# Attention scores of each head in a PSUM bank of their own, and the turned probabilities in two banks

## The chip, the cores and the metric

One core of a Trainium2 chip runs the kernel. The time is the device time of one execution in microseconds (us). The kernel before has a median of 2364.11 us in three runs (2362.43 to 2365.06).

## What is computed

One hybrid encoder layer is applied with the same weights to two sequences of 256 and 1024 tokens, of width 1024. A windowed attention branch (16 query heads in 4 groups, head width 64, window 128) and a bidirectional mLSTM branch run on the same normalised input; a gated merge, a projection, and a gated feed-forward follow. The attention is all that the change touches:

```python
def block_fn(args):
    j, qj, kj, vj = args
    kpos = j * BLOCK - BLOCK + jnp.arange(3 * BLOCK)
    valid = in_window & ((kpos >= 0) & (kpos < S))[None, :]
    s = jnp.einsum('bqgrd,bkgd->bgrqk', qj.astype(F32), kj.astype(F32)) * scale + alibi
    s = jnp.where(valid, s, -jnp.inf)
    sink_col = jnp.broadcast_to(sink_g[None, :, :, None, None], s.shape[:-1] + (1,))
    p = jax.nn.softmax(jnp.concatenate([s, sink_col], axis=-1), axis=-1)[..., :-1]
    o = jnp.einsum('bgrqk,bkgd->bqgrd', p, vj.astype(F32))
    return o.astype(qj.dtype)
```

## The kernel before

Tokens stand on the free axis in most of the program; both sequences are joined into 1280 tokens, ten blocks of 128. A group of four query heads with its one key and value head, and one mLSTM head, are done together: this is "a head" below, `h` = 0 to 3. For each, `mlstm(h)` runs first and `attend(h)` after it. Beside the attention of heads 0 to 2 TensorE (PE) computes dense input products of the next mLSTM head, two groups in each block (`M_BESIDE`); beside head 3 it computes late gate products (`late_group`) in block 0 and products of the mLSTM branch (`branch_m`, table `B_BESIDE`) from block 1 on.

Numbers are carried as a high part and a low part (a "split"): the high part is a rounded copy that ScalarE (ACT) writes, the low part the difference that VectorE (DVE) subtracts.

A block `j` sees two key blocks at a sequence's edge (`j` = 0, 1, 2, 9) and three inside (`j` = 3 to 8). For a block, in the order of the data:

- PE, `a_scores(j)` (matmul at L3653): for each of the four query heads `r`, a product with the high and with the low keys. `S_AT` says at which column of three joined PSUM banks (2, 3, 4) a head's scores begin: at 0, 384, 768 and 1152. A bank holds 512 columns, so heads 1 and 2 lie across a bank's end and are written in two pieces each.
- DVE, `scores_max(j)` (L2727, L2730): adds the distance term and takes the maximum; `exp_bias(j)` (L2735 to L2740). It writes `prob`, so it waits until the probabilities of block `j - 1` have been turned (`a_t`).
- ACT, `exps(j)` (L2340), then DVE, `normalise(j)` (L2752), one count of `a_p` for each query head.
- PE, `a_turn(j)` (transposes at L3673): each key block's probabilities are turned, four transposes into one bank; banks 6, 7 and 5 for the first, second and third key block (`TURN_BANK`). The scores of the next block stand between the second and the third turn (in edge blocks after the second). Bank 5 is also where the values' product is summed, so before the third turn PE waits for `a_o`, the last read of bank 5 by block `j - 1`.
- ACT, `evac_pt(j)` (L2348) writes the high part of each turned block, and DVE, `split_probs(j)` (L2813), the low part, after `scores_max(j + 1)` and `exp_bias(j + 1)`.
- PE: the dense groups beside the block, then `a_values(j)` (L3686, L3687) into bank 5.
- ACT, `evac_o(j)` (L2375), reads one half of the sum, DVE, `add_out(j)` (L2819), adds the other half and counts `a_o`.

Each engine does its own list in the order written. On ACT `evac_pt(j)` stands behind `evac_o(j - 1)` and what follows that: in heads 0 to 2, from block 4 to 7, two tanh gates (`gate_o`, L2168); in head 3, behind `evac_o(2)`, the eight copies of `ym_hi(2)` (L2397). In block 0 of head 3 the eight copies of `ym_hi(0)` stand just ahead of `evac_pt(0)`, and `ym_hi(1)`, two `evac_late` (L2093) and `evac_o(0)` follow `exps(1)`. GpSimd (POOL) takes the low parts of `ym_hi` (L1525) before `branch_m` may use them.

Of the kernel before, what the change touches and what calls it, by code (L numbers as in the profile page):

```python
# [24 lines left out]
P = 128  # L25
# [4 lines left out]
NB = T // P  # L30
# [3 lines left out]
HD = 64  # L34
QPG = 4
# [116 lines left out]
RAW = {"B11": 9, "B21": 10, "B22": 11, "B12": 12}  # L152


S_AT = [3 * P * r for r in range(4)]


COLS_AT = 9
# [41 lines left out]

LAST_AHEAD = 3

TURN_BANK = [6, 7, 5]

CHUNKS = [(0, 256), (256, 768), (768, T)]

# [243 lines left out]
def lin(f, h):  # L450

    if isinstance(h, int):
        return f(h)
    a, b = f(0), f(1)
    assert f(2) == 2 * b - a
    return h * (b - a) + a if b != a else a


def build(nc, w, wdn, xt, cols, bvo, sink, outs):
# [36 lines left out]
    prob_h = at("prob_h", 159808, [P, 3, QPG * P], F32R)  # L496
    prob_l = at("prob_l", 199392, [P, 3, QPG * P], F32R)
    ya_st = at("ya_st", 165952, [HD, QPG, P])
# [121 lines left out]
    ps = nc.alloc_psum_tensor("ps", [P, 8, 512], F32)  # L620
# [73 lines left out]
    a_t = sem("a_probs_transposed")  # L694
# [164 lines left out]
    def kblocks(j):  # L859
        lo, hi = seq_of(j)  # L860
        return list(range(max(lo, j - 1), min(hi, j + 2)))
# [5 lines left out]
    def tiles_before(j):  # L867

        return sum(len(kblocks(n)) for n in range(j))

    def score_at(j, r):

# [67 lines left out]
    with ctx_block as block:  # L940
# [1116 lines left out]
        def _(act):  # L2057
# [285 lines left out]

            def evac_pt(j, h):

                act.wait_ge(a_t, lin(lambda k: NB * k + j + 1, h))
                for n in range(len(kblocks(j))):
                    nc.scalar.activation(prob_h[:, n], ps[:, TURN_BANK[n], :], ACT.Identity).then_inc(a_pt, 1)  # L2348

            def split_keys(h):  # L2350
# [19 lines left out]
            def evac_o(j, h):  # L2370

                act.wait_ge(a_v, lin(lambda k: NB * k + j + 1, h))
                if j > 0:
                    act.wait_ge(s_ya, lin(lambda k: 16 * (NB * k + j), h))
                nc.scalar.activation(ya_st[:], ps[HD:P, 5, :].rearrange("p (r t) -> p r t", r=QPG),  # L2375
                                     ACT.Copy).then_inc(a_oc, 1)

            def store_o(j, h):
# [99 lines left out]
        def _(dve):  # L2478
            V = nc.vector
# [238 lines left out]
            def scores_max(j, h):  # L2718

                kb = kblocks(j)  # L2720
                a, b = (kb[0] - j + 1) * P, (kb[-1] - j + 2) * P
                dve.wait_ge(a_s_done, lin(lambda k: NB * k + j + 1, h))
                flat = ps[:, 2:5, :].rearrange("p b t -> p (b t)")
                if j > 0:
                    dve.wait_ge(a_t, lin(lambda k: NB * k + j, h))
                for r in range(QPG):
                    V.scalar_tensor_tensor(prob[:, r, a:b], absrel[:, a:b], slope8[:, bass.ds(h * QPG + r, 1)],  # L2727
                                           flat[:, score_at(j, r) + a:score_at(j, r) + b], ALU.mult, ALU.add)
                dve.drain()
                V.tensor_reduce(small[:, 16:20], prob[:, :, a:b], AX.X, ALU.max)  # L2730
# [72 lines left out]
                                           q_st[j > 0][rows, odd].bitcast(F32), ALU.subtract)  # L2803
                last.then_inc(a_ql, 1)

            def split_probs(j, h):

                if j == 0:
                    for s in range(2):
                        dve.wait_ge(s_gs[s], gates_stored(h))  # L2810
                for n in range(len(kblocks(j))):
                    dve.wait_ge(a_pt, lin(lambda k: tiles_before(NB) * k + tiles_before(j) + n + 1, h))
                    last = V.tensor_tensor(prob_l[:, n], ps[:, TURN_BANK[n], :], prob_h[:, n].bitcast(F32),  # L2813
                                           ALU.subtract)
                last.then_inc(a_pl, 1)

            def add_out(j, h):
                dve.wait_ge(a_oc, lin(lambda k: NB * k + j + 1, h))
                V.tensor_tensor(ya_st[:], ya_st[:], ps[0:HD, 5, :].rearrange("p (r t) -> p r t", r=QPG),  # L2819
                                ALU.add).then_inc(a_o, 1)  # L2820

            def attend(h, dense):
                dve.drain()
                split_keys(0, h)
                split_query(0, h)
                split_values(h)
                dve.wait_ge(m_y, lin(lambda k: 5 * (k + 1), h))
                scores_max(0, h)
                exp_bias(0, h)
                split_keys(1, h)  # L2830
                split_query(1, h)
                normalise(0, h)
                for j in range(NB):

                    if j + 1 < NB:
                        scores_max(j + 1, h)
                        exp_bias(j + 1, h)
                    ahead = B_BESIDE[j][:1] if not dense and len(B_BESIDE[j]) == 3 else []
                    for n in ahead:
                        gate_product(n)  # L2840
                    split_probs(j, h)
                    if j + 2 < NB:
                        split_query(j + 2, h)
                    vo = [g - 12 for g in M_BESIDE[j] if dense and g >= 12]
                    for blk in vo[:1]:
                        evac_vo(blk, h, 1)
                    if j + 1 < NB:
                        normalise(j + 1, h)
                    for blk in vo[1:]:
                        evac_vo(blk, h, 1)  # L2850
                    if not dense and j == 0:
                        ym_lo_last()
                    if not dense:
                        for n in B_BESIDE[j][len(ahead):]:
                            gate_product(n)
                    add_out(j, h)
                if not dense:
                    ya_lo(0)
                    gate_product(NBR - 2)
                    ya_lo(1, range(3))  # L2860
                    gate_product(NBR - 1)
                    ya_lo(1, range(3, KT))
                    ya_lo(2)

                dve.wait_ge(m_ye, lin(lambda k: 5 * (k + 1), h))
# [493 lines left out]
        def _(pe):  # L3359
# [278 lines left out]
            def a_scores(j, h):  # L3638

                kb = kblocks(j)  # L3640
                a, b = (kb[0] - j + 1) * P, (kb[-1] - j + 2) * P
                if j in (0, NB_A):
                    pe.wait_ge(a_kl, 2 * h + 1 + (j > 0))
                if j:
                    pe.wait_ge(a_m, lin(lambda k: NB * k + j, h))
                pe.wait_ge(a_ql, lin(lambda k: NB * k + j + 1, h))
                for r in range(QPG):
                    lo = score_at(j, r) + a
                    while lo < score_at(j, r) + b:
                        hi = min(score_at(j, r) + b, (lo // 512 + 1) * 512)  # L3650
                        k0 = (j - 1) * P + lo - score_at(j, r)
                        for n, keys in enumerate((kk_h, kk_l)):
                            ins = mm(ps[:, 2 + lo // 512, lo % 512:lo % 512 + hi - lo], q_st[j > 0][:, r % 2, r // 2],  # L3653
                                     keys[:, k0:k0 + hi - lo], start=n == 0, stop=n == 1)
                        lo = hi
                ins.then_inc(a_s_done, 1)

            def a_turn(j, h):


                if j == 0:
                    pe.wait_ge(a_av, lin(lambda k: k + 1, h))
                kb = kblocks(j)
                for n, blk in enumerate(kb):
                    o = (blk - j + 1) * P
                    if n == 2:
                        if j + 1 < NB:
                            a_scores(j + 1, h)
                        pe.wait_ge(a_o, lin(lambda k: NB * k + j, h))
                    for r in range(QPG):  # L3670
                        if n == 0:
                            pe.wait_ge(a_p, QPG * (NB * h + j) + r + 1)
                        ins = nc.tensor.transpose(ps[:, TURN_BANK[n], r * P:(r + 1) * P], prob[:, r, o:o + P], ident[:])  # L3673
                ins.then_inc(a_t, 1)
                if len(kb) < 3 and j + 1 < NB:
                    a_scores(j + 1, h)

            def a_values(j, h):

                pe.wait_ge(a_pl, lin(lambda k: NB * k + j + 1, h))  # L3680
                kb = kblocks(j)
                if len(kb) < 3 and j > 0:
                    pe.wait_ge(a_o, lin(lambda k: NB * k + j, h))
                for n, blk in enumerate(kb):
                    vals = v_block(blk).rearrange("p s e -> p (s e)")
                    mm(ps[:, 5, :], vals, prob_h[:, n], start=n == 0, stop=False)  # L3686
                    ins = mm(ps[:, 5, :], vals, prob_l[:, n], start=False, stop=n == len(kb) - 1)  # L3687
                ins.then_inc(a_v, 1)

            def branch_m(n):  # L3690
# [526 lines left out]
```

## Time and profile before

| | before |
|---|---|
| median of the runs | 2364.11 us (2362.43 to 2365.06) |
| the profiled execution's own time | 2362.85 us |
| its span, first to last instruction | 2361.0 us |
| PE busy | 2328.4 us, 99% of the span |
| DVE, ACT, POOL busy | 65%, 39%, 54% |
| share of PE in the chain that ended last | 81% |
| scores, L3653, in 28 to 53% of the span | 416 matmuls |
| granted TensorE clock, mean | 0.999 |

A matmul's row shows a start and a modelled end; the next one starts before that end, so the pace of PE is read from start to start, and a busy share of 99% does not say that it ran at its peak. In a timeline, rows of one kind that follow each other are merged into one (x8), with the time from the first start to the last end.

### The profile page before, as it was taken

Reading aid. Unit: us, or ns where it says so; the run is one execution under the profiler, and the core shown is the slowest. Engines: PE = TensorE matmul, PEld = TensorE weight load, DVE = VectorE, ACT = ScalarE, POOL = GpSimd, SP = SyncE. Lnnn points to the kernel's source line nnn. Section 1 sums busy time; section 2 is a strip of 40 time slices with the busy share of each in tenths; the row PEclk is TensorE's granted clock in tenths of the full one; section 3 lists DMA queues with packets and bytes.
Section 4 is the critical chain, followed back from the end, with each engine's and each line's share of the span. In section 5 each row is a group of like instructions: output and inputs, shape, how many; then the busy total and the mean of one; then the engine's idle time right before and its main releaser. Section 6 shows DMA issues by size and latency. Waiting matters only on the chain.

```text
span 2361.0 us, 37054 instructions
## 1 busy us (share of the span) xinstructions
PE 2328.4 (99%) x13662; PEld 2104.9 (89%) x13662; DVE 1544.0 (65%) x2731; ACT 909.3 (39%) x1886; POOL 1276.2 (54%) x1548
## 2 busy tenths in 40 slices
PE   7999999999999999999999999999999999999998
PEld 6888888888888888888888899999999999989887
DVE  6734467555674547755786633999878788866447
ACT  5212444224442244324644112554433334542433
POOL 3365522555225651345443548797555555976677
PEclk9999999999999999999999999999999999999999
DMA  3132211321113211223454443332444434488873
GB/s 140 52 110 90 71 37 28 113 92 51 37 41 110 92 52 32 73 82 125 130 165 163 140 152 124 125 111 90 156 146 141 157 130 151 136 287 272 283 232 121
DMA packets 186956, 285.64 MB, mean 121 GB/s; under 512 B 14344, under 2 KB 126824, under 8 KB 186776
## 3 DMA queue, kind: packets, MB, share of 16 engines
q1 hardware_dynamic: 139320, 241.97, 31.1%
q10 hardware_dynamic: 47456, 41.31, 5.8%
q8 instruction: 109, 1.79, 0.3%
q14 instruction: 71, 0.58, 0.1%
HBM read 203.46 MB, written 79.68 MB: 120 GB/s over the span
## 4 chain that ended last, share of the span: by engine, by line
PE 81%; DVE 8%; DMA 4%; DVEq 2%; POOL 2%; ACT 1%; issue 1%; SPq 1%; ACTq 0%; POOLq 0%
PE ps L3373 15%; PE ps L3374 15%; PE ps L3375 15%; PE ps L3388 3%; PE ps L3384 3%; PE ps L3385 3%; PE ps L3438 3%; PE ps L3439 3%; PE ps L3440 3%; PE ps L3653 2%; PE ps L3673 2%; PE ps L3555 2%; PE ps L3944 2%; PE ps L3946 2%; PE ps L3945 2%; DMA weight_sum_scratch<-s_stage 1%
## 5 line engine op out<-in xcount | busy, mean ns | idle before, releaser
L3373 PE MATMUL ps<-ht_h,unit_h 128*128 128x512 f32 (+1 forms) x1408 | 502.5, 357 | 1.5 <-POOL unit_l L1434 0.8
L3375 PE MATMUL ps<-ht_h,unit_l 128*128 128x512 f32 (+1 forms) x1408 | 498.4, 354 | 0.0
L3374 PE MATMUL ps<-ht_l,unit_h 128*128 128x512 f32 (+1 forms) x1408 | 498.3, 354 | 0.0
L1412 POOL TENSOR_TENSOR unit_h<-unit_raw,colt 128x256 fp32r<-128x256 f32 x320 | 209.4, 684 | 275.5 <-DMA unit_raw<-w 275.1
L3373 PEld LDWEIGHTS ps<-ht_h,unit_h 128*128 128x128 f32 x1408 | 266.1, 189 | 37.9 <-POOL unit_l L1434 1.8
L3375 PEld LDWEIGHTS ps<-ht_h,unit_l 128*128 128x128 f32 x1408 | 265.9, 189 | 37.5
L3374 PEld LDWEIGHTS ps<-ht_l,unit_h 128*128 128x128 f32 x1408 | 266.2, 189 | 35.0 <-issue 0.2
L1416 POOL TENSOR_TENSOR unit_l<-unit_raw,unit_h 128x256 fp32r<-128x256 f32 x320 | 246.7, 802 | 11.7 <-issue 0.4
L1584 POOL TENSOR_TENSOR unit_l<-unit_raw,unit_h 128x256 fp32r<-128x256 f32 x164 | 158.5, 991 | 92.5 <-DVE unit_raw L3023 92.5
L1584 POOL TENSOR_TENSOR sum_l<-sum_raw,sum_h 128x256 fp32r<-128x256 f32 x132 | 139.5, 1076 | 86.8 <-DVE sum_raw L3030 74.7
L1505 POOL TENSOR_TENSOR v_high<-v_raw,colt 128x256 fp32r<-128x256 f32 x40 | 27.0, 675 | 231.5 <-DVE o_st L2526 231.5
L2340 ACT ACTIVATE prob<-prob,small 128x384 f32<-128x384 f32 (+1 forms) x160 | 89.8, 563 | 112.4 <-DVE small L2740 112.3
L1624 POOL TENSOR_TENSOR block_l<-block_raw,block_h 128x256 fp32r<-128x256 f32 x120 | 106.7, 925 | 47.9 <-ACT block_h L1955 47.8
L3384 PE MATMUL ps<-operands,unit_h 128*128 128x320 f32 x420 | 125.3, 310 | 0.2 <-DVE kept_products L3179 0.2
L3385 PE MATMUL ps<-operands,unit_h 128*128 128x320 f32 x420 | 124.7, 309 | 0.0
L3438 PE MATMUL ps<-unit_h,ht_h 128*128 128x512 f32 x312 | 123.2, 395 | 0.0
L2727 DVE SCALAR_TENSOR_TENSOR prob<-absrel,slope,ps 128x384 f32<-128x384 f32 (+1 forms) x160 | 79.0, 556 | 65.8 <-PE ps L3673 38.2
L3440 PE MATMUL ps<-unit_h,ht_l 128*128 128x512 f32 x312 | 121.6, 390 | 0.0
L3439 PE MATMUL ps<-unit_l,ht_h 128*128 128x512 f32 x312 | 121.5, 389 | 0.0
L3122 DVE TENSOR_TENSOR side<-side_raw,side 128x1536 fp32r<-128x1536 f32 (+2 forms) x40 | 65.7, 1676 | 53.2 <-ACT side L1860 53.2
L3373 PE MATMUL ps<-operands,unit_h 128*128 128x320 f32 x320 | 99.1, 310 | 0.2
L3374 PE MATMUL ps<-operands,unit_h 128*128 128x320 f32 x320 | 98.9, 309 | 0.0
(441 smaller groups left out, 6414.0 us busy)
## 6 DMA issues: line engine op xcount, KB each, us to landing
unit_raw<-w SPq DMA_DIRECT2D x149, 512.0 KB, 3.7
bw<-exponent_rows_scratch ACTq DMA_DIRECT2D x40, 256.0 KB, 3.6
down_raw<-wdn SPq DMA_DIRECT2D x24, 384.0 KB, 4.5
side_raw<-side_sum_scratch SPq DMA_DIRECT2D x24, 384.0 KB, 6.4
block_raw<-weight_sum_scratch SPq DMA_DIRECT2D x16, 576.0 KB, 4.3
gate_scratch<-g_st SPq DMA_DIRECT2D x28, 256.0 KB, 2.2
stage<-f_scratch SPq DMA_DIRECT2D x28, 256.0 KB, 3.0
side_sum_scratch<-stage SPq DMA_DIRECT2D x14, 512.0 KB, 2.9
```

The source lines that it names most:

```text
L1412: nc.gpsimd.tensor_tensor(unit_h[:, slot, k:k + 2], unit_raw[:, slot, k:k + 2], one_col.unsqueeze(2).to_broadcast([P, 2, P]), ALU.mult)
L1416: last = nc.gpsimd.tensor_tensor(unit_l[:, slot, k:k + 2], unit_raw[:, slot, k:k + 2], unit_h[:, slot, k:k + 2].bitcast(F32), ALU.subtract)
L1584: last = nc.gpsimd.tensor_tensor(lo[:, k:k + 2], raw[:, k:k + 2], hi[:, k:k + 2].bitcast(F32), ALU.subtract)
L1624: last = nc.gpsimd.tensor_tensor(blk_l[n][:, a:b], blk_raw[n][:, a:b], blk_h[n][:, a:b].bitcast(F32), ALU.subtract)
L3373: mm(out_ap, wh, hi(k + k_first), start=first and k == 0, stop=False, skip_group_check=skip)
L3374: mm(out_ap, wh, lo(k + k_first), start=False, stop=False, skip_group_check=skip)
L3375: ins = mm(out_ap, wl, hi(k + k_first), start=False, stop=last and k == kts - 1, skip_group_check=skip)
L3384: mm(out_ap, unit[0](k), hi(k), start=first and k == 0, stop=False, skip_group_check=skip)
L3385: mm(out_ap, unit[0](k), lo(k), start=False, stop=False, skip_group_check=skip)
L3438: mm(ps[:, bank, :], ht_h[:, k, t], unit_h[:, 0:4, k], start=k == 0, stop=False)
L3439: mm(ps[:, bank, :], ht_h[:, k, t], unit_l[:, 0:4, k], start=False, stop=False)
L3440: ins = mm(ps[:, bank, :], ht_l[:, k, t], unit_h[:, 0:4, k], start=False, stop=k == KT - 1)
```

## The change

The scores of the four query heads begin at columns 0, 512, 1024 and 1536 of four joined banks (2 to 5). The turns go to banks 7, 6 and 7, and the values' sum to bank 6. So the third turn waits until DVE has split the first, which left the same bank; the second turn waits for `a_o` of the block before; the next block's scores stand between the first and the second turn, in edge blocks too. `a_t` and `a_pl` count twice in a block (after the first turn or split, and after the last), ACT takes the first turned block on the first count, and DVE's split of the first block moves ahead of `scores_max(j + 1)`.

```diff
-S_AT = [3 * P * r for r in range(4)]
+S_AT = [4 * P * r for r in range(4)]
-TURN_BANK = [6, 7, 5]
+TURN_BANK = [7, 6, 7]
+VALUE_BANK = 6
+    def turns_done(j, h, whole):
+        return 2 * (NB * h + j) + 1 + whole
             def evac_pt(j, h):
-                act.wait_ge(a_t, lin(lambda k: NB * k + j + 1, h))
                 for n in range(len(kblocks(j))):
+                    if n < 2:
+                        act.wait_ge(a_t, turns_done(j, h, n > 0))
                     nc.scalar.activation(prob_h[:, n], ps[:, TURN_BANK[n], :], ACT.Identity).then_inc(a_pt, 1)
...
                 if j > 0:
-                    dve.wait_ge(a_t, lin(lambda k: NB * k + j, h))
+                    dve.wait_ge(a_t, turns_done(j - 1, h, True))
...
-            def split_probs(j, h):
-                if j == 0:
+            def split_probs(j, h, first):
+                if j == 0 and first:
...
-                for n in range(len(kblocks(j))):
+                for n in range(1) if first else range(1, len(kblocks(j))):
...
                 for j in range(NB):
+                    split_probs(j, h, True)
                     if j + 1 < NB:
                         scores_max(j + 1, h)
                         exp_bias(j + 1, h)
...
-                    split_probs(j, h)
+                    split_probs(j, h, False)
...
                 for n, blk in enumerate(kb):
                     o = (blk - j + 1) * P
-                    if n == 2:
+                    if n == 1:
                         if j + 1 < NB:
                             a_scores(j + 1, h)
-                        pe.wait_ge(a_o, lin(lambda k: NB * k + j, h))
+                        if j:
+                            pe.wait_ge(a_o, lin(lambda k: NB * k + j, h))
+                    elif n == 2:
+                        pe.wait_ge(a_pl, turns_done(j, h, False))
...
+                    if n == 0:
+                        ins.then_inc(a_t, 1)
                 ins.then_inc(a_t, 1)
-                if len(kb) < 3 and j + 1 < NB:
-                    a_scores(j + 1, h)
             def a_values(j, h):
-                pe.wait_ge(a_pl, lin(lambda k: NB * k + j + 1, h))
+                pe.wait_ge(a_pl, turns_done(j, h, True))
                 kb = kblocks(j)
-                if len(kb) < 3 and j > 0:
-                    pe.wait_ge(a_o, lin(lambda k: NB * k + j, h))
```

PE at the turn of block 4 in head 0, before. `ident,prob` is a transpose of four (one key block) or eight, `kk_h` and `kk_l` are the high and low keys, `unit_h,ht_h` is the dense group behind it; two pairs of 256 columns and one of 128 are left out:

```order
L3673 MATMUL ps<-ident,prob 128x128 x8
L3653 MATMUL ps<-kk_h,q_st 128x384
L3653 MATMUL ps<-kk_l,q_st 128x384
L3653 MATMUL ps<-kk_h,q_st 128x128
L3653 MATMUL ps<-kk_l,q_st 128x128
...
L3653 MATMUL ps<-kk_h,q_st 128x384
L3653 MATMUL ps<-kk_l,q_st 128x384
L3673 MATMUL ps<-ident,prob 128x128 x4
L3438 MATMUL ps<-unit_h,ht_h 128x512
```

The same place now:

```order
L3682 MATMUL ps<-ident,prob 128x128 x4
L3659 MATMUL ps<-kk_h,q_st 128x384
L3659 MATMUL ps<-kk_l,q_st 128x384
L3659 MATMUL ps<-kk_h,q_st 128x384
L3659 MATMUL ps<-kk_l,q_st 128x384
...
L3682 MATMUL ps<-ident,prob 128x128 x8
L3444 MATMUL ps<-unit_h,ht_h 128x512
```

Twelve score matmuls became eight of 384 columns, and the second turn moved from ahead of them to behind them.

DVE at the end of block 0 and in block 1 of head 3, before (`ht_l<-y_c` is the low part of `ym_hi(1)`, `ya_st` is `add_out(0)`):

```order
L2752 TENSOR_SCALAR prob<-prob,small 128x256 x4
L2727 SCALAR_TENSOR_TENSOR prob<-absrel,slope_75,ps 128x256 x4
L2730 TENSOR_REDUCE small<-prob 128x4
L2735 SCALAR_TENSOR_TENSOR small<-sinks,small 128x4
L2738 TENSOR_SCALAR small<-small 128x4
L2740 TENSOR_TENSOR small<-sinks,small 128x4
L2813 TENSOR_TENSOR prob_l<-ps,prob_h 128x512 x2
```

And now:

```order
L2757 TENSOR_SCALAR prob<-prob,small 128x256 x4
L2818 TENSOR_TENSOR prob_l<-ps,prob_h 128x512
L2732 SCALAR_TENSOR_TENSOR prob<-absrel,slope_75,ps 128x256 x4
L2735 TENSOR_REDUCE small<-prob 128x4
L2740 SCALAR_TENSOR_TENSOR small<-sinks,small 128x4
L2743 TENSOR_SCALAR small<-small 128x4
L2745 TENSOR_TENSOR small<-sinks,small 128x4
L2818 TENSOR_TENSOR prob_l<-ps,prob_h 128x512
```

One split of the two moved ahead of the next block's maximum, so that this waits for ACT's copy of the first turned block.

## Rows read from the trace of the kernel before

**Rows 1.** The page, part 1: busy time, share of the span, instructions.

```profile
PE 2328.4 (99%) x13662; PEld 2104.9 (89%) x13662; DVE 1544.0 (65%) x2731; ACT 909.3 (39%) x1886; POOL 1276.2 (54%) x1548
```

**Rows 2.** Waits of PE, 284 to 1275 us: waiter, releaser: total us, times, longest.

```profile
PE ps L3673 <- DVE prob L2752: 0.9, 4, 0.2
```

**Rows 3.** Timeline of PE, turn of block 5, head 0: start us, us, instruction.

```profile
362.62 1.03 PE L3673 MATMUL ps<-ident,prob 128*128 128x128 f32 x8
363.40 0.42 PE L3653 MATMUL ps<-kk_h,q_st 128*128 128x384 f32 x1
363.66 0.33 PE L3653 MATMUL ps<-kk_l,q_st 128*128 128x384 f32 x1
363.83 0.22 PE L3653 MATMUL ps<-kk_h,q_st 128*128 128x128 f32 x1
...
364.00 0.33 PE L3653 MATMUL ps<-kk_h,q_st 128*128 128x256 f32 x1
...
364.93 0.34 PE L3653 MATMUL ps<-kk_l,q_st 128*128 128x384 f32 x1
365.10 0.60 PE L3673 MATMUL ps<-ident,prob 128*128 128x128 f32 x4
```

**Rows 4.** Timeline of ACT, the same turn.

```profile
362.81 0.59 ACT L2375 ACTIVATE ya_st<-ps 64x512 f32<-64x512 f32 x1 [4.82 <-PE ps L3687]
363.31 0.71 ACT L2168 ACTIVATE o_st<-o_st 128x256 f32<-128x256 f32 x2
365.74 0.60 ACT L2348 ACTIVATE prob_h<-ps 128x512 fp32r<-128x512 f32 x1 [1.72 <-PE ps L3673]
```

**Rows 5.** Timeline of DVE, the same turn.

```profile
363.44 0.68 DVE L2819 TENSOR_TENSOR ya_st<-ya_st,ps 64x512 f32<-64x512 f32 x1 [1.25 <-ACT ya_st L2375]
...
370.81 1.88 DVE L2813 TENSOR_TENSOR prob_l<-ps,prob_h 128x512 fp32r<-128x512 f32 x3
```

**Rows 6.** Timeline of PE, edge scores in the turn of block 8, head 0.

```profile
409.08 0.36 PE L3653 MATMUL ps<-kk_h,q_st 128*128 128x256 f32 x1
...
410.11 0.60 PE L3673 MATMUL ps<-ident,prob 128*128 128x128 f32 x4
```

**Rows 7.** Timeline of PE, turn of block 9, head 0.

```profile
420.19 0.76 PE L3673 MATMUL ps<-ident,prob 128*128 128x128 f32 x5 [0.21 <-DVE prob L2752]
420.71 0.48 PE L3438 MATMUL ps<-unit_h,ht_h 128*128 128x512 f32 x1
```

**Rows 8.** Timeline of DVE, the same turn.

```profile
420.32 0.68 DVE L2819 TENSOR_TENSOR ya_st<-ya_st,ps 64x512 f32<-64x512 f32 x1 [0.18 <-ACT ya_st L2375]
```

**Rows 9.** Timelines of ACT, DVE, PE and POOL, blocks 0 and 1 of head 3.

```profile
1128.23 1.07 ACT L2348 ACTIVATE prob_h<-ps 128x512 fp32r<-128x512 f32 x2
...
1126.95 1.66 DVE L2727 SCALAR_TENSOR_TENSOR prob<-absrel,slope,ps 128x256 f32<-128x256 f32 x4 [5.09 <-PE ps L3653]
...
1139.75 0.67 DVE L2819 TENSOR_TENSOR ya_st<-ya_st,ps 64x512 f32<-64x512 f32 x1
...
1138.56 1.03 PE L3673 MATMUL ps<-ident,prob 128*128 128x128 f32 x8
...
1144.07 0.47 PE L3373 MATMUL ps<-ht_h,unit_h 128*128 128x512 f32 x1 [0.66 <-issue]
...
1134.22 9.70 POOL L1525 TENSOR_TENSOR ht_l<-y_c,ht_h 128x256 fp32r<-128x256 f32 x10 [1.07 <-ACT ht_h L2397]
```

**Rows 10.** Timelines of ACT and PE, turn of block 3, head 3.

```profile
1168.44 2.70 ACT L2397 ACTIVATE ht_h<-y_c 128x512 fp32r<-128x512 f32 x5
...
1172.73 1.58 ACT L2348 ACTIVATE prob_h<-ps 128x512 fp32r<-128x512 f32 x3
...
1170.24 0.60 PE L3673 MATMUL ps<-ident,prob 128*128 128x128 f32 x4
```

**Rows 11.** PE at the program's end: timeline, then stretches with busy us and granted clock.

```profile
2350.70 0.70 PE L4113 MATMUL ps<-sq_y,ones 128*128 128x256 f32 x2 [0.53 <-ACT sq_y L1948]
...
2355.00:2358.00 3.00, 0.00 (x0) 0.62 0.30 103
```

More of the change, by code:

```diff
@@ L2374, in evac_o @@
                     act.wait_ge(s_ya, lin(lambda k: 16 * (NB * k + j), h))
-                nc.scalar.activation(ya_st[:], ps[HD:P, 5, :].rearrange("p (r t) -> p r t", r=QPG),
+                nc.scalar.activation(ya_st[:], ps[HD:P, VALUE_BANK, :].rearrange("p (r t) -> p r t", r=QPG),
                                      ACT.Copy).then_inc(a_oc, 1)
@@ L2722, in scores_max @@
                 dve.wait_ge(a_s_done, lin(lambda k: NB * k + j + 1, h))
-                flat = ps[:, 2:5, :].rearrange("p b t -> p (b t)")
+                flat = ps[:, 2:6, :].rearrange("p b t -> p (b t)")
                 if j > 0:
-                    dve.wait_ge(a_t, lin(lambda k: NB * k + j, h))
+                    dve.wait_ge(a_t, turns_done(j - 1, h, True))
                 for r in range(QPG):
@@ L2818, in add_out @@
                 dve.wait_ge(a_oc, lin(lambda k: NB * k + j + 1, h))
-                V.tensor_tensor(ya_st[:], ya_st[:], ps[0:HD, 5, :].rearrange("p (r t) -> p r t", r=QPG),
+                V.tensor_tensor(ya_st[:], ya_st[:], ps[0:HD, VALUE_BANK, :].rearrange("p (r t) -> p r t", r=QPG),
                                 ALU.add).then_inc(a_o, 1)
@@ L3673, in a_turn @@
                         ins = nc.tensor.transpose(ps[:, TURN_BANK[n], r * P:(r + 1) * P], prob[:, r, o:o + P], ident[:])
+                    if n == 0:
+                        ins.then_inc(a_t, 1)
                 ins.then_inc(a_t, 1)
-                if len(kb) < 3 and j + 1 < NB:
-                    a_scores(j + 1, h)
             def a_values(j, h):
-                pe.wait_ge(a_pl, lin(lambda k: NB * k + j + 1, h))
+                pe.wait_ge(a_pl, turns_done(j, h, True))
                 kb = kblocks(j)
-                if len(kb) < 3 and j > 0:
-                    pe.wait_ge(a_o, lin(lambda k: NB * k + j, h))
                 for n, blk in enumerate(kb):
                     vals = v_block(blk).rearrange("p s e -> p (s e)")
-                    mm(ps[:, 5, :], vals, prob_h[:, n], start=n == 0, stop=False)
-                    ins = mm(ps[:, 5, :], vals, prob_l[:, n], start=False, stop=n == len(kb) - 1)
+                    mm(ps[:, VALUE_BANK, :], vals, prob_h[:, n], start=n == 0, stop=False)
+                    ins = mm(ps[:, VALUE_BANK, :], vals, prob_l[:, n], start=False, stop=n == len(kb) - 1)
                 ins.then_inc(a_v, 1)
```

## The prediction

> **What bounds the kernel now.** I read the page first: PE is busy in 99% of the span [rows 1]. That says only that it seldom stands, so I asked next for its waits over the four attention stages (284 to 1275 us): for the probabilities it waited 0.9 us in all, four times [rows 2], and for no other step of the attention. The reader is to see that the turns and scores have no slack to win: PE goes through them at its own pace, so time is won by giving PE less to do and lost by every wait that PE meets. The third view is the timeline of one turn. There PE's pace is start to start [rows 3]: the turn begins at 362.62, two turns of four transposes last until 363.40, twelve score matmuls until 365.10. ACT and DVE at the same turn show how soon the new waits could end [rows 4, 5].
>
> **What is removed.** The scores of an inner block take 365.10 - 363.40 = 1.70 us [rows 3]. A 384-column matmul takes 0.17 us (363.66 to 363.83, 364.93 to 365.10), the first behind a transpose 0.26. A pair of 128 columns takes 0.17 (363.83 to 364.00), where the edge scores do 256 columns in 0.13 (eight from 409.08 to 410.11 [rows 6]): the short pieces are what costs. Eight matmuls of 384 give 0.26 + 7 x 0.174 = 1.48, so 0.22 less. It holds for blocks 3 to 8 of four heads, 24 times: **-5.3 us**. No row shows eight in a run; bounds are nothing, if they go no faster than the pieces did, and 0.34, if none takes over 0.17. The Trainium skill, "TensorE: Matmul & The Clock Gate", section "Wait — 56ns, not 53.3ns?", gives a matmul N columns at 2.4 GHz plus about 2.5 ns whatever its length. By that, four matmuls fewer would save 10 ns a block, 0.24 us in all, and the sum below would end 5.1 us higher. The trace does not agree: 128 columns twice take 0.17 us [rows 3], not 0.112.
>
> **What is added: waits of PE.** I set 0 at the first transpose of a turn. Four transposes and the step to the scores take 0.36 (half of 0.78, less a little), so with inner scores PE reaches the second turn at 0.36 + 1.48 = 1.84 and the third at 1.84 + 0.44 = 2.28; with edge scores (1.03, 409.08 to 410.11 [rows 6]) at 1.39 and 1.83.
>
> The second turn waits for `add_out` of the block before. It ends at 364.12 - 362.62 = 1.50 [rows 3, 5]; with 0.06 to PE (an estimate, twice the step from ACT's end at 363.40 to DVE's start at 363.44) that is 1.56. So inner turns 2 to 7 are covered, and block 1 waits 0.17. In block 9 nothing lies between the turns: `add_out` ends at 421.00 [rows 8], the second turn stands at 421.06 where it stood at 420.35 (0.36 ahead of 420.71) [rows 7]: 0.71.
>
> The third turn waits for ACT's copy and DVE's split of the first. Where ACT has only `evac_o` ahead, the copy ends before `add_out` does, and the split (1.88 / 3 = 0.63, 0.68 for a single one) ends at 1.50 + 0.63 and reaches PE at 2.19: covered at 2.28, in blocks 3 and 4 of heads 0 to 2 and 4 to 7 of head 3. Behind two tanh gates, in blocks 5 to 8 of heads 0 to 2, ACT is free at 363.92, that is 1.30 (the gates end at 364.02, and one ACT instruction starts 0.1 before the last one's end, as 363.31 against 363.40) [rows 4]; copy 0.60, split 0.68, steps 0.03 and 0.06: 2.68. Blocks 5, 6 and 7 wait 2.68 - 2.28 = 0.40 each, block 8, with edge scores, 2.68 - 1.83 = 0.85. A restart costs 0.05 more (five transposes take 0.52 behind a wait [rows 7], eight 0.78). Bounds of such a wait: nothing, if the split lands 0.4 earlier, and 0.9, if DVE is held as long again.
>
> Heads 0 to 2, each: block 1 0.17, blocks 5 to 7 1.20, block 8 0.85, block 9 0.71, six restarts 0.30, together 3.2; less 6 x 0.22 = 1.3: +1.9, three times **+5.7 us**.
>
> **Head 3** has two places where ACT is far behind when the first turn comes.
> Block 0: ACT copies it only at 1128.23, after `ym_hi(0)` [rows 9]; this cost nothing, since DVE went on with `scores_max(1)` at 1126.95. Now DVE's first split stands ahead of it: copy to 1128.83, split 0.6, and `scores_max(1)` begins at 1129.45, **2.5 later**. Behind it on ACT, `exps(1)` and then `ym_hi(1)` move by as much, so do `evac_o(0)` and `add_out(0)` (1139.75, now 1142.25, ended 1142.92). PE, whose turn of block 1 starts at 1138.56, reaches its second turn at 1139.95 and stands 3 us, to 1142.98. After it come 0.44 and a branch product of 24 matmuls of 256 columns, 24 x 0.13 = 3.1, to 1146.5; the next one needs POOL's low parts, which ended at 1143.92 and now at 1146.42, and begins at 1146.57 where it began at 1144.07: +2.5, bounds 1.5 (if DVE makes up part of it) and 3.1.
> Block 3: the eight copies of `ym_hi(2)` stand between `evac_o(2)` and `evac_pt(3)`, and ACT reaches the latter at 1172.73 [rows 10]. Copy 0.60, split 0.68, steps 0.09: the third turn at 1174.10, where PE, whose turn began 2.48 before 1170.24, would be at 1167.76 + 2.28 = 1170.04. It stands 4.0 us, bounds 3.6 and 4.6.
> The others: block 8 2.19 - 1.83 = 0.36, block 9 1.56 - 0.44 = 1.12, restarts 0.2. Sum 2.5 + 4.0 + 0.36 + 1.12 + 0.2 = 8.2, less 1.3: **+6.9 us**.
>
> What costs nothing: DVE's moved split lies where DVE stood, between `add_out` and `scores_max`, and shortens the way to the next probabilities by 0.6; PE waited for those 0.9 us in all [rows 2], so it wins little. No DMA moves.
>
> **The sum** is 5.7 + 6.9 = +12.6 us on the profiled execution's own 2362.85 us: 2375.4. The median of the runs stands 1.3 above that execution, which I leave inside the range. I call less than 0.2% (4.7 us) no change; that is about what a measurement of this kernel can tell.
>
> **The rivals.**
> 1. The waits are covered after all, and the kernel is faster. The place is the third turn of blocks 5 to 8; its price is 0.40 to 0.85 each, and the point that decides is whether the first split lands 0.40 us earlier than I put it, before PE's own arrival. For it: ACT gets its count after four transposes, and DVE is idle. Against: both engines do their lists in order, and gates and `add_out` stand ahead [rows 4, 5]. It also needs head 3 free of its two long waits. With all waits at nothing only -5.3 is left: 2357.5.
> 2. The long waits of head 3 do not come, as ACT reaches the first turn as early as in the other heads. Against it stands ACT's order in rows 9 and 10. Head 3 then costs 0.17 + 0.36 + 1.12 + 0.15 - 1.3 = +0.5, the sum is +6.2: 2369.1.
> 3. The clock falls in head 3's long stand. At the program's end the last matmul ended at 2351.40, and the stretch from 2355 to 2358 has a granted clock of 0.62, a mix of full (2.4 GHz) and half (1.2 GHz): full for 0.7 us of it, so it fell 4.3 us after the last matmul [rows 11]. The stand of 4.0 us is just shorter. If the clock falls, the branch product behind it (3.1 us) takes twice as long: 2378.5. The Trainium skill, the same page, section "What's actually happening", has the clock gated down by default and released by activity; by that rule, too, the stand would cost this much, and the end of the trace agrees with it.
> 4. Waits feed on each other in head 3 (later probabilities for block 2, later branch operands), 3 to 5 us more: about 2379.5.
> 5. Eight matmuls take as long as the twelve did, since something else than the pieces sets the pace there, and the waits come all the same: 12.6 + 5.3 = +17.9, 2380.8. No row shows eight in a run; against it stands the pair at 0.17 where 256 columns take 0.13. The skill's rule of the first part would come out here.
>
> **How the numbers follow.** My forecast 0.57, rival 1 0.05, rival 2 0.12, rival 3 0.14, rival 4 0.08, rival 5 0.04. The likeliest case gives 2375.4. Its bounds (waits of blocks 5 to 8 and block 0 of head 3, the pieces' price) spread it by some 3 us to either side, 2372 to 2379. Rival 2 reaches down to 2369 and rival 3 lies inside; rivals 1 and 5 and the outer part of 4 stay out: 2369 to 2380. Faster is rival 1 alone, 0.04; no change holds the lower half of rival 2 and a little more, 0.09; slower the rest, 0.87.
>
> **What would show it.** In the profile after: 13662 - 96 = 13566 matmuls at most; inner scores at 1.4 to 1.5 us; a new wait of PE at the transposes for DVE's split, some 0.4 us in blocks 5 to 7 and 0.85 in block 8 of heads 0 to 2; one of about 4 us in block 3 of head 3; a wait for `add_out` of 0.7 to 1.1 us in block 9 of each head and of 3 us in block 1 of head 3. I am wrong if PE reaches the third turns without standing, if ACT copies the first turn ahead of the gates or of `ym_hi(2)`, or if the eight matmuls take 1.7 us again.

## The result, and the profile after

| | before | after |
|---|---|---|
| median of the runs, us | 2363.93 (2362.43 to 2365.06, 6 runs) | 2380.72 (2379.25 to 2382.55, 6 runs) |
| ratio to before | | 1.0073 [1.0062, 1.0084] |
| the profiled execution's own time | 2362.85 | 2382.46 |
| its span | 2361.0 | 2380.6 |
| granted TensorE clock, mean | 0.999 | 0.997 |

The change costs 16.8 us. The forecast was 2375.4, in a range of 2369.0 to 2380.0; the direction came out, the time lies 0.7 above the range. The two profiled executions differ by more, 19.6 us, since the one of after lies 1.7 above its median and the one of before 1.1 below.

Part 1 of the page of after (busy time, share of the span, instructions):

```profile
PE 2332.4 (98%) x13566; PEld 2102.6 (88%) x13566; DVE 1551.8 (65%) x2731; ACT 914.3 (38%) x1886; POOL 1279.4 (54%) x1548
```

The 96 matmuls are gone, and yet PE is busy for 4 us more than in [rows 1]: a first hint that some matmuls ran at a lower clock. The waits of PE in the attention stages (280 to 1300 us: waiter, releaser, total us, times, longest), where [rows 2] had one row for the attention, with 0.9 us:

```profile
PE ps L3682 <- DVE prob_l L2818: 9.0, 13, 3.9
PE ps L3682 <- DVE ya_st L2824: 6.7, 5, 2.8
PE ps L3682 <- DVE prob L2757: 0.7, 3, 0.3
```

The first row is the third turn's wait for the split of the first: 13 times, that is blocks 5 to 8 of heads 0 to 2 and block 3 of head 3 (the 3.9). The second is the wait for `add_out`. The places are those of the forecast. PE in the turn of block 5, head 0, to set beside [rows 3]:

```profile
362.08 0.60 PE L3682 MATMUL ps<-ident,prob 128*128 128x128 f32 x4
362.43 0.42 PE L3659 MATMUL ps<-kk_h,q_st 128*128 128x384 f32 x1
362.69 0.34 PE L3659 MATMUL ps<-kk_l,q_st 128*128 128x384 f32 x1
...
363.93 0.60 PE L3682 MATMUL ps<-ident,prob 128*128 128x128 f32 x4
364.89 0.66 PE L3682 MATMUL ps<-ident,prob 128*128 128x128 f32 x4 [0.36 <-DVE prob_l L2818]
365.30 0.48 PE L3444 MATMUL ps<-unit_h,ht_h 128*128 128x512 f32 x1
```

The eight scores take 363.93 - 362.43 = 1.50 us, where the twelve took 1.70. The third turn begins at 2.81 after the turn's start. Without the wait PE would be there at 2.28, as it is in block 4. The whole turn takes 3.22 (to 365.30) where it took 2.84. ACT in the same turn ([rows 4]):

```profile
362.28 0.60 ACT L2380 ACTIVATE ya_st<-ps 64x512 f32<-64x512 f32 x1 [4.82 <-PE ps L3694]
362.77 0.71 ACT L2172 ACTIVATE o_st<-o_st 128x256 f32<-128x256 f32 x2
363.51 0.60 ACT L2353 ACTIVATE prob_h<-ps 128x512 fp32r<-128x512 f32 x1
```

And DVE ([rows 5]):

```profile
362.91 0.68 DVE L2824 TENSOR_TENSOR ya_st<-ya_st,ps 64x512 f32<-64x512 f32 x1 [1.25 <-ACT ya_st L2380]
364.14 0.69 DVE L2818 TENSOR_TENSOR prob_l<-ps,prob_h 128x512 fp32r<-128x512 f32 x1 [0.56 <-ACT prob_h L2353]
```

The first turned block is there by 362.68, but its copy starts at 363.51, behind the two gates; the split follows, and 0.06 after its end PE goes on.

Blocks 0 and 1 of head 3 ([rows 9]), in timelines of PE, ACT, DVE and POOL:

```profile
1151.32 0.66 PE L3682 MATMUL ps<-ident,prob 128*128 128x128 f32 x4 [2.84 <-DVE ya_st L2824]
...
1136.53 1.06 ACT L2353 ACTIVATE prob_h<-ps 128x512 fp32r<-128x512 f32 x2
...
1144.39 4.26 ACT L2402 ACTIVATE ht_h<-y_c 128x512 fp32r<-128x512 f32 x8
...
1137.24 0.69 DVE L2818 TENSOR_TENSOR prob_l<-ps,prob_h 128x512 fp32r<-128x512 f32 x1 [7.07 <-ACT prob_h L2353]
1137.85 1.65 DVE L2732 SCALAR_TENSOR_TENSOR prob<-absrel,slope,ps 128x256 f32<-128x256 f32 x4
...
1150.59 0.67 DVE L2824 TENSOR_TENSOR ya_st<-ya_st,ps 64x512 f32<-64x512 f32 x1
```

DVE's first split now waits for ACT's copy (DVE stands 7.07 us, where it stood 5.09), and `scores_max(1)` begins 4.62 after the first transpose of block 0 (1137.85 - 1133.23), where it began 2.02 after it (1126.95 - 1124.93). These 2.6 us come back 13 us later as PE's stand of 2.84. Block 3 of head 3 ([rows 10]):

```profile
1179.55 0.60 PE L3682 MATMUL ps<-ident,prob 128*128 128x128 f32 x4
...
1185.90 0.78 PE L3682 MATMUL ps<-ident,prob 128*128 128x128 f32 x4 [3.92 <-DVE prob_l L2818]
...
1186.91 0.41 PE L3381 MATMUL ps<-ht_h,unit_l 128*128 128x256 f32 x1
1187.12 0.41 PE L3379 MATMUL ps<-ht_h,unit_h 128*128 128x256 f32 x1
...
1190.06 0.28 PE L3379 MATMUL ps<-ht_h,unit_h 128*128 128x256 f32 x1
1190.17 0.28 PE L3380 MATMUL ps<-ht_l,unit_h 128*128 128x256 f32 x1
...
1180.24 4.26 ACT L2402 ACTIVATE ht_h<-y_c 128x512 fp32r<-128x512 f32 x8
1184.52 0.60 ACT L2353 ACTIVATE prob_h<-ps 128x512 fp32r<-128x512 f32 x1
```

After the stand a matmul of 256 columns takes 0.21 from start to start (1186.91 to 1187.12), from 1190 on 0.11 to 0.12. Stretches of PE around both stands (busy us and count, granted clock, DMA share, GB/s):

```profile
1147.00:1152.00 5.00, 2.16 (x19) 1.00 0.35 86
1152.20:1155.50 3.30, 3.30 (x18) 0.50 0.76 283
...
1179.00:1186.20 7.20, 3.28 (x23) 1.00 0.38 115
1186.30:1189.70 3.40, 3.40 (x19) 0.50 0.21 41
1190.00:1195.00 5.00, 5.00 (x27) 1.00 0.09 30
```

Behind each of the two stands the granted clock is 0.50, that is 1.2 GHz, for some 3.4 us. The kernel before has no such stretch but the one at its end [rows 11].

The turns, from the first transpose's start to the start of the first dense matmul, in the profiled executions (forecasts are the sum's own terms: wait, restart, less 0.22 where the scores are inner ones):

| turn | before, us | after, us | difference | forecast |
|---|---|---|---|---|
| heads 0 to 2, block 1 | 1.82 | 1.97 | +0.15 | +0.22 |
| blocks 5, 6, 7 | 2.84 | 3.22 | +0.38 | +0.23 |
| block 8 | 2.18 | 3.22 | +1.04 | +0.90 |
| block 9 | 1.22 | 1.97 | +0.75 | +0.76 |
| head 3, block 1 | 1.82 | 4.87 | +3.05 | +3.05 |
| block 3 | 2.85 | 6.79 | +3.94 | +3.83 |
| block 8 | 2.18 | 2.61 | +0.43 | +0.41 |
| block 9 | 0.79 | 1.97 | +1.18 | +1.17 |

Over all 40 turns that is +15.19, of which +7.31 in heads 0 to 2 (forecast +5.7) and +7.88 in head 3. Another 3.1 lies behind the turns. The dense work of block 1 of head 3, from its first matmul to the first one of the values' product, took 12.12 us and takes 12.79, though PE's wait for POOL of 0.66 in it [rows 9] is gone; in block 3 it took 11.30 and takes 12.78. The other 0.9 comes in small parts from the edge blocks 0 to 2 of each head: there the first dense matmul now follows transposes instead of scores, and takes 0.20 from start to start where it took 0.11 (310.73 to 310.93 in block 1 of head 0, before 310.75 to 310.86). The last 1.4 of the 19.6 between the two profiled executions lies outside the heads' attention; the change doesn't touch it.

### The profile page after: what moved, and what is told of

It is laid out like the page before. It is cut to its first block, busy times and chain, and to the rows that moved or that the text cites. A ratio compares the mean times of both kernels' runs of the same rounds, so it can differ in the third digit from the quotient of the medians.

```text
span 2380.6 us, 36850 instructions
## 1 busy us (share of the span) xinstructions
PE 2332.4 (98%) x13566; PEld 2102.6 (88%) x13566; DVE 1551.8 (65%) x2731; ACT 914.3 (38%) x1886; POOL 1279.4 (54%) x1548
## 4 chain that ended last, share of the span: by engine, by line
PE 82%; DVE 8%; ACT 3%; DVEq 2%; DMA 2%; POOL 2%; issue 1%; SPq 0%; ACTq 0%; POOLq 0%
PE ps L3379 15%; PE ps L3381 15%; PE ps L3380 15%; PE ps L3446 3%; PE ps L3444 3%; PE ps L3445 3%; PE ps L3394 3%; PE ps L3390 3%; PE ps L3391 3%; PE ps L3951 3%; PE ps L3952 3%; PE ps L3953 3%; PE ps L3561 2%; PE ps L3682 2%; PE ps L3659 1%
```

## The experiments

The theory (A in what follows): the forecast's waits are there, each set by what stands ahead of the copy or the split on ACT and DVE, and on top of them the clock falls behind both long stands of head 3. The rivals: the scores gained less than they seem to (the waits were there whatever the scores took), and the time behind head 3's stands is a matter of late operands, not of the clock. The kernel before was timed again beside the experiments and had medians of 2363.48 us (beside 1 to 4) and 2363.83 (beside 5 to 7); ratios are to these, and a difference between two medians is good to half a microsecond at best.

**1. The scores packed again**, everything else as changed:

```diff
-S_AT = [4 * P * r for r in range(4)]
+S_AT = [3 * P * r for r in range(4)]
```

> The change with the scores back at 0, 384, 768, 1152 (twelve matmuls for an inner block), turns and values' sum still in two banks. Theory A (four matmuls fewer win 0.2 us, but only where the third turn does not wait for the split anyway, 14 of 24 turns): inner scores 1.70 us, third turns of blocks 5 to 7 of heads 0 to 2 still 2.81 us behind the first transpose, median 2380.7 + 14 x 0.2 = 2383.5. Rival (the pieces cost nothing): 2380.7. Rival (the gain holds 24 times): 2385.8.

Measured: 2384.77 (2383.46 to 2385.76), ratio 1.0090 [1.0075, 1.0105], that is 4.0 above the changed kernel's median. This lies between the 2383.5 of theory A and the 2385.8 of the rival that has the gain 24 times, so the trace has to tell them apart. In it the second turn behind inner scores comes at 2.06 instead of 1.84. There are 14 such turns without a wait for the split at their end (blocks 2 to 4 of heads 0 to 2, five of head 3). Ten of them grow by 0.21 to 0.23; the other four (block 3 of heads 1 and 2, blocks 6 and 7 of head 3) have late probabilities or a late split in one or both executions, and change by -0.36 to +0.64. In the remaining ten turns (blocks 5 to 7 of heads 0 to 2, block 3 of head 3) the third turn still comes at 2.81 and 6.35, and the wait shrinks in its place:

```profile
PE ps L3682 <- DVE prob_l L2818: 6.4, 10, 3.7
```

All turns together are 2.7 us longer, of the 4.0 between the medians. So the gain is real: 0.22 for each block's eight matmuls, and where a wait stands behind them it only makes the wait longer. The Trainium skill, "TensorE: Matmul & The Clock Gate", section "Wait — 56ns, not 53.3ns?", has a matmul cost its columns and about 2.5 ns, by which four matmuls fewer would give 0.01. Both traces, with 0.22, speak against using it for these short pieces.

**2. PE kept at work in head 3's two stands.** In blocks 1 and 3 of head 3 PE computes the next block's scores twice more, just ahead of the wait. This adds work that is thrown away, and no engine's order changes:

```diff
                     if n == 1:
                         if j + 1 < NB:
                             a_scores(j + 1, h)
+                        if h == HEADS - 1 and j == 1:
+                            a_again(j + 1, 2)
...
                     elif n == 2:
+                        if h == HEADS - 1 and j == 3:
+                            a_again(j + 1, 2)
                         pe.wait_ge(a_pl, turns_done(j, h, False))
```

> The change, and in head 3 PE computes the next block's scores twice over again where it would stand: in block 1 ahead of the second turn, in block 3 ahead of the third. The result is the same; the waits stay. Theory A (the two stands let the clock fall to half for 3.4 us each, 1.3 to 1.7 us lost each): turns as long as in the change, 4.9 and 6.8 us, but the granted clock stays at 1.00 behind them, and the median falls by about 3 us to 2377.7. Theory B (what is longer behind the two turns is a wait for data or a slower memory, not the clock): no gain, 2380.7.

Measured: 2377.04 (2376.22 to 2377.15), ratio 1.0057 [1.0042, 1.0072]. The two turns are as long as before the edit (4.89 and 6.77), but the work behind them takes 11.60 and 11.29, where it took 12.79 and 12.78. The same stretches, with the same columns:

```profile
1152.20:1155.60 3.40, 3.31 (x27) 1.00 0.84 302
1178.60:1185.40 6.80, 5.69 (x38) 1.00 0.35 96
1185.50:1189.50 4.00, 4.00 (x32) 1.00 0.19 39
```

The clock is full, and behind the second stand 32 matmuls fit into 4.0 us where 19 took 3.4. This settles the second rival: no operand came earlier, and the time went nonetheless. The falls cost 1.19 + 1.49 = 2.7 us in the traces; the medians differ by 3.7, and the slowest of these runs is 2.1 below the fastest run of the change.

**3. `ym_hi(2)` behind the copies of block 3** on ACT, instead of ahead of them:

```diff
                     evac_pt(j, h)
+                    if not dense and j == 3:
+                        ym_hi(2)
...
-                    if not dense and j == 2:
-                        ym_hi(2)
```

> The change with ym_hi(2) of head 3 moved behind evac_pt(3) on ACT. Theory A (ACT's eight copies ahead of the first turned block are the whole of the 3.9 us that block 3 of head 3 lost, and their stand the cause of the second clock fall): third turn at 2.3 us instead of 6.35, one fall of the clock fewer, 3.9 + 1.5 less: 2375.3. Theory B (the split is late for another reason, or the copies are then missed by the branch products): 2379 to 2381.

Measured: 2376.38 (2375.57 to 2377.19), ratio 1.0054 [1.0039, 1.0069]: 4.3 less. PE and ACT in that turn:

```profile
1179.33 0.60 PE L3682 MATMUL ps<-ident,prob 128*128 128x128 f32 x4
...
1181.18 1.04 PE L3682 MATMUL ps<-ident,prob 128*128 128x128 f32 x8
...
1180.15 0.60 ACT L2353 ACTIVATE prob_h<-ps 128x512 fp32r<-128x512 f32 x1
...
1183.23 4.27 ACT L2402 ACTIVATE ht_h<-y_c 128x512 fp32r<-128x512 f32 x8
```

The second and third turn are one run of eight again, the turn takes 2.64 instead of 6.79, and the half clock behind it is gone. Something is given back: the eight copies now stand ahead of the next block's exponentials, and block 4's turn, which waits for its probabilities, takes 3.39 (2.63 after the change).

**4. The early split only in inner blocks**, so that in edge blocks `scores_max(j + 1)` stands first again on DVE:

```diff
-                    split_probs(j, h, True)
+                    early = len(kblocks(j)) == 3
+                    if early:
+                        split_probs(j, h, True)
...
+                    if not early:
+                        split_probs(j, h, True)
                     split_probs(j, h, False)
```

> The change with DVE's split of the first turned block put back behind the next block's maximum in blocks of two key blocks (0, 1, 2 and 9), which have no third turn. Theory A (the moved split made block 1's maximum wait for ACT in head 3, and all that follows): second turn of block 1 of head 3 at 1.9 to 2.1 us instead of 4.46, POOL's wait of 0.7 us behind it back, no clock fall there; 3.05 - 0.5 - 0.6 + 1.3 less: 2377.5. Theory B (the copies of ym_hi(1) hold PE whatever DVE does): no gain, 2380.7.

Measured: 2377.65 (2376.86 to 2378.90), ratio 1.0060 [1.0043, 1.0077]: 3.1 less. Block 1 of head 3:

```profile
1149.02 0.66 PE L3686 MATMUL ps<-ident,prob 128*128 128x128 f32 x4 [0.37 <-DVE ya_st L2824]
```

The stand of 2.84 is 0.37 now, and the turn takes 2.33; the clock stays full there, and the work behind it takes 11.62. The order on DVE alone made all of this stand but 0.37. PE's wait for POOL's low parts, which theory A had come back with 0.7, does not come back. In block 3, which the edit doesn't touch, the half clock lasted twice as long in this execution (1181.4 to 1188.2), and turn and work behind it took 1.1 us more than after the change, so the edit by itself is worth about a microsecond more than the run shows.

**5. The gates of a block behind the first copy of the next** on ACT:

```diff
-            def evac_pt(j, h):
+            def evac_pt(j, h, gates=()):
                 for n in range(len(kblocks(j))):
+                    if n == 1:
+                        for blk in gates:
+                            gate_o(blk, h + 1)
...
-                    evac_pt(j, h)
+                    old = [g - 12 for g in M_BESIDE[j - 1] if j and dense and g >= 12]
+                    evac_pt(j, h, old if len(old) == 2 else ())
...
-                    if len(vo) == 2:
-                        gate_o(vo[0], h + 1)
-                        gate_o(vo[1], h + 1)
```

> The change with the two tanh gates of blocks 4 to 7 (heads 0 to 2) moved on ACT from behind evac_o to behind the copy of the next block's first turn. Theory A (the gates set when the first split lands): third turns of blocks 5 to 7 at 2.28 us instead of 2.81, turns 2.64 instead of 3.22; block 8's third turn at 2.2; 9 x 0.58 + 3 x 0.6 = 7.0 less: 2373.7. Theory B (DVE's add_out or the copy itself sets it): third turns stay at 2.7 to 2.8, 2380.7.

Measured: 2374.39 (2373.71 to 2374.98), ratio 1.0045 [1.0030, 1.0060]: 6.3 less. ACT in the turn of block 5, head 0, then PE's waits of the attention stages:

```profile
362.45 0.60 ACT L2383 ACTIVATE ya_st<-ps 64x512 f32<-64x512 f32 x1 [4.82 <-PE ps L3695]
363.07 0.60 ACT L2356 ACTIVATE prob_h<-ps 128x512 fp32r<-128x512 f32 x1
363.56 0.71 ACT L2172 ACTIVATE o_st<-o_st 128x256 f32<-128x256 f32 x2
```

```profile
PE ps L3683 <- DVE ya_st L2825: 6.7, 5, 2.8
PE ps L3683 <- DVE prob_l L2819: 3.9, 1, 3.9
```

The copy starts 0.82 after the turn's start instead of 1.43, and twelve of the thirteen waits are gone: blocks 5 to 7 take 2.64, block 8 2.61. That is 9 x 0.58 + 3 x 0.61 = 7.1 us; a longer half clock in block 1 of head 3 (6.8 us in this execution) took 1.1 of it.

**6. Other banks in blocks 1, 8 and 9.** There the next scores are edge scores or none, and banks 4 and 5 hold none that are still wanted. The turns go to banks 7, 5 and 4, the wait for the split falls away, and the wait for `a_o` moves to the values:

```diff
+def turn_bank(j, n):
+    return ([7, 5, 4] if j in FREE else TURN_BANK)[n]
+FREE = (1, NB - 2, NB - 1)
...
-                        if j:
+                        if j and j not in FREE:
                             pe.wait_ge(a_o, lin(lambda k: NB * k + j, h))
-                    elif n == 2:
+                    elif n == 2 and j not in FREE:
                         pe.wait_ge(a_pl, turns_done(j, h, False))
...
                 pe.wait_ge(a_pl, turns_done(j, h, True))
+                if j in FREE:
+                    pe.wait_ge(a_o, lin(lambda k: NB * k + j, h))
```

> The change with three banks for the turns of blocks 1, 8 and 9 (7, 5 and 4), beside which no inner scores are computed, so that banks 4 and 5 are free; the wait for add_out moves ahead of the values there. Theory A (the shared bank is what costs at the sequence's edges): block 8 back to 2.2 us, blocks 1 and 9 to 1.8 and 0.8 to 1.2; 3 x 0.15 + 3 x 1.04 + 0.43 + 3 x 0.75 + 1.18 = 7.4 less, and in head 3 block 1 the stand of 3 us goes in part, POOL's low parts still hold the second branch product: 2371 to 2373. Theory B (PE would meet another wait there, for probabilities or values): 2377 or more.

Measured: 2373.81 (2373.48 to 2375.66), ratio 1.0045 [1.0031, 1.0058]: 6.9 less, a little short of what was expected. Block 8 takes 2.17 again in every head, block 1 1.74 in heads 0 to 2, block 9 of head 3 0.79. Two places give less. PE, no longer held in block 8, comes to block 9 of heads 0 to 2 before its probabilities, as it did in [rows 7] (these turns take 1.66, 1.09 and 1.09); and in block 1 of head 3 the stand only moved behind the scores: the turn is 1.9 shorter and the work behind it 2.3 longer. PE, then POOL:

```profile
421.15 1.03 PE L3690 MATMUL ps<-ident,prob 128*128 128x128 f32 x6 [0.40 <-DVE prob L2765]
...
1144.53 0.39 PE L3387 MATMUL ps<-ht_h,unit_h 128*128 128x256 f32 x1 [0.95 <-ACT gw L2105]
...
1149.61 0.57 PE L3387 MATMUL ps<-ht_h,unit_h 128*128 128x512 f32 x1 [1.94 <-issue]
1149.98 0.63 PE L3388 MATMUL ps<-ht_l,unit_h 128*128 128x512 f32 x1
1150.41 0.63 PE L3389 MATMUL ps<-ht_h,unit_l 128*128 128x512 f32 x1
...
1139.77 9.69 POOL L1537 TENSOR_TENSOR ht_l<-y_c,ht_h 128x256 fp32r<-128x256 f32 x10 [3.64 <-ACT ht_h L2410]
```

PE meets ACT's late `evac_late` (0.95) and then POOL's late low parts (1.94, to 1149.61; POOL ends them at 1149.46); the second had been expected, the first not. So the bank was only where PE met this delay, not its cause; what was late were ACT's exponentials and `ym_hi(1)`, behind DVE's early split. The rows also show that the clock fell here: 512 columns take 0.43 from start to start (1149.98 to 1150.41), where the kernel before needs 0.23 for them.

**7. Edits 3 to 6 together:**

> The change with all four repairs: the copies of ym_hi(2) and the gates behind the first turn's copy, the early split in inner blocks alone, three turn banks in blocks 1, 8 and 9. Theory A (nothing but the shared bank's waits and the two falls of the clock took the gain): no wait of PE at the transposes but for probabilities, clock 1.00 throughout, 24 x 0.2 us less than before: 2358.7, ratio 0.998. Theory B (gain and waits are joined, for instance since ACT falls behind elsewhere): 2364 or more.

Measured: 2361.35 (2359.16 to 2363.43, 11 runs) against 2363.83 (2362.18 to 2365.57, 15 runs) of the kernel before, ratio 0.9989 [0.9980, 0.9998]. It beats both kernels, the one before by 2.5 us, about half of what was expected. Its mean clock is 0.999, with no half clock before the end. The one wait left at its transposes:

```profile
PE ps L3695 <- DVE prob L2766: 1.6, 5, 0.4
```

The turns sum to -4.27: inner ones take 2.64 where they took 2.84, but blocks 3 and 9 of some heads and block 4 of head 3 (3.41, where it took 3.00) are at the pace of the probabilities, which no quicker score helps. Another 0.9 of it is lost behind the turns of the edge blocks, where dense matmuls follow transposes, as after the change (in block 1 of heads 0 to 2 the dense work takes 8.42 instead of 8.33), and 0.6 between the attention of heads 2 and 3, a stretch that takes 134.3 to 135.0 in the profiled executions of the nine kernels.

## Why the prediction was right, and where it failed

- **Direction and mechanism: right.** Waits that the shared banks add outweigh the gain in the scores, and they stand where the forecast put them. Experiments 3 to 6 remove them one after another by changing only what stands ahead in a list, or the bank.
- **The gain of the scores: right.** 1.50 was measured for 1.48 forecast, and taking it back cost 0.22 in each turn that waited for nothing.
- **Head 3: the waits right to about 0.1 us.** The turn of block 1 grew by the 3.05 forecast, that of block 3 by 3.94 for 3.83. The net of +2.5 for block 1, with POOL's wait gone in exchange, shows in the run with PE kept busy: 3.07 in the turn, less 12.12 - 11.60 behind it, is 2.55.
- **The failed step: the clock.** The sum left it out by "The stand of 4.0 us is just shorter", a comparison with the one fall in the trace, 4.3 us after the program's last matmul [rows 11]. One idle stretch at the end was no bound for a stand in the middle: in the ten falls that the traces of the change and of experiments 1 to 6 hold there, the clock went down 1.9 to 4.8 us after PE had stopped. It fell at the stand of 3.9 and, where the forecast didn't look for it, at the one of 2.8 too. Rival 3 had the mechanism, with 0.14 and one place, and a price too high: it took twice the 3.1 us of a branch product, but half of what runs in 3.4 us at half clock is done nonetheless, so that a fall cost 1.2 to 1.5. Two of them are 2.7 us in the traces, shown by experiment 2.
- **A term too small: the third turn's wait in blocks 5 to 8 of heads 0 to 2.** The step "ACT is free at 363.92, that is 1.30" let the copy start 0.1 before the gates' end. It started 0.03 after (363.48 to 363.51), at 1.43, and the third turn came at 2.81 instead of 2.68. 12 x 0.13 = 1.6 us, as much as the difference between +7.31 and +5.7. The other misses in these heads cancel, by luck: block 3, at the pace of its probabilities, was 0.5 longer than forecast in the three heads together, blocks 0, 1 and 2 were 0.7 shorter.
- **The sum** with both mended: 12.6 + 1.6 + 2.7 = 16.9 us, for 16.8 measured between the medians. That it is so close is in part luck. The two profiled executions, from which the terms are read, differ by 19.6; of the 2.7 that the sum doesn't hold, 1.4 lies outside the attention, 0.9 behind the turns of the edge blocks, and 0.5 in the turns of head 3, most of it in block 7, which waited for its probabilities.
- **The range** took the errors one at a time. On the profiled execution's own 2362.85 us the mended sum gives 2379.7, still inside; but that execution stands 1.1 below the median of six runs, which the forecast left "inside the range" although it moves the time one way only, and with it the time passes the top.

## What to carry to other kernels

A PSUM bank that two steps of one turn share ties PE to whatever stands ahead in the ordered lists of the engines that empty it: price the wait by those lists at each place, and before giving up the bank plan move the emptying ahead of work without a deadline, or use banks that are idle at the edges. In this kernel, where PE is busy 99% of the time, new stands of 2.8 and 3.9 us cost their own length and then 1.2 and 1.5 us at half clock; so look for every new stand of PE, price the clock with it, and ask what PE could do in it. A gain that is counted in each block is worth nothing in those that then wait for something else, so count the blocks without a wait.

## What the runs showed of the hardware that was not expected

- **The clock fell around stands of 1.9 to 3.9 us, and the fall is not tied to the stand's end.** After the stand of 2.84 us it fell 0.8 us after PE had resumed (1152.16 against 1151.32), after that of 3.92 0.4 after (1186.29 against 1185.90). In experiment 1 it fell 1.4 after PE had resumed (1154.59 against 1153.14), in experiments 4 and 5 1.0 before (1181.40 against 1182.44, 1142.64 against 1143.62); the last of these is 1.9 after PE had stopped. With other banks (experiment 6) the last stand before the first fall was of 1.94 us, with one of 0.95 some 3 us earlier, and the clock went down at 1149.82, 0.2 after PE had resumed. The stretches at 1.2 GHz lasted 3.4 us, in two of the ten falls 6.8 (experiments 4 and 5). Stands of 0.37 us (experiment 4) and of 1.0 and 1.1 us (experiment 2) brought none in blocks 1 and 3 of head 3. What sets the moment of a fall is not shown by these runs. The Trainium skill, "TensorE: Matmul & The Clock Gate", section "What's actually happening", has the clock down by default and released by activity, and these runs agree with that much: it fell where PE stood and came back while PE was at work.
- **An ACT copy with a wait ahead of it started 0.03 us after the last instruction's end**, though what it waited for was long done (363.51 after 363.48, the transposes by 362.68); the gates, with no wait, start 0.1 before that end, as in [rows 4].
